# Two mixing layers in fp32 on one core: 22 of 50 weight slots as seven quarter-size products for eight, and attention's rounds in another order

## The chip, the core and the metric

The kernel runs on one core of a Trainium2 chip, in fp32. A core has five engines with queues of their own: TensorE (PE, matrix products into PSUM), VectorE (DVE), ScalarE (ACT), GpSimd (POOL) and SyncE (SP), which here only starts DMA transfers. They meet through semaphores: an instruction raises one when it ends, another engine waits for its value. The metric is the device time of one execution in microseconds, as the median of several. Less is better.

## The reference

The program is one block of another kind (a recurrent branch and latent attention) and then two equal layers over 272 tokens (16 learned ones and 256 of the input) of width 1024. The change concerns only the first part of these two layers, which I call the mixing stage:

```python
for l in range(2):
    n = rms_norm(h, mix_norm_g[l])
    q, k, v, qi, ki, wi, xr, yg, cv, gt = split(n @ w_in[l])
    q = rotary(rms_norm(q)); k = rotary(rms_norm(k)); qi = rotary(qi); ki = rotary(ki)
    # 8 small heads score the keys: sum_h wi[h] * relu(qi[h] . ki); the best 64 keys of a query stay
    attn = attention(q, k, v, kept keys)      # 8 heads of 128 over 2 groups of keys
    rnn  = scan(a_t * h + b_t) * gelu(yg)     # gates from two block-diagonal products of conv4(xr)
    cnv  = silu(layer_norm(conv31(cv_a * sigmoid(cv_g))))
    g_attn, g_rnn, g_conv = split(sigmoid(gt))
    merged = g_attn * (attn @ w_o_attn) + g_rnn * (rnn @ w_o_rnn) + g_conv * (cnv @ w_o_conv)
    h = h + merged @ w_out
    f = rms_norm(h, ffn_norm_g[l])
    h = h + (silu(f @ w_gate) * (f @ w_up)) @ w_down
```

conv31 and conv4 are causal convolutions of each channel by itself, over 31 and 4 tokens. Layer 1 leaves out the 16 learned tokens wherever only queries are needed, so its queries, gates, branches and output run over 256 columns.

## The kernel before

Features lie on the 128 partitions and tokens along the columns: a matrix of width 1024 is 8 tiles of 128 x 272. All weights come as one stream of slots of 1 MB (1024 rows by 256 outputs) in a ring of four (the order in LSTREAM; SyncE issues a slot's transfer at L501 once the slot four before it is used up, `slot_free`). One slot gives two output tiles of 128 features. `project` (L525 to L537) computes them plainly: for each tile 8 matmuls of 128x128 weights with 272 (or 256) columns, accumulated in one PSUM bank; four banks rotate, and ScalarE's `keep` (L769) copies each tile out.

The mixing stage of a layer takes 50 such slots after the small ones for qi, ki and wi: 8 for the inputs of the long convolution, 4 for q, 1 for k, 1 for v, 4 for xr, 4 for yg, 12 for the three gates, and then 4 each for the recurrent, the attention and the convolution branch and the output. TensorE's program is one fixed list. Between projections it has the small products: the index heads' logits; the sums of squares of heads (L605); the transposes of v; the 16 block-diagonal gate inputs of the recurrence (L618, between the YG and the gate projections); then attention in rounds (six in layer 0, four in layer 1): scores of four heads (L630), two or three gate slots, transposes of the weights (L637), and so on. The product with V comes after all rounds (L649: 8 heads, three key tiles each, 272 columns). Last come 32 tiles of branches and output (L676).

ScalarE copies, applies sigmoid, gelu, relu, exp and silu (the convolution's norm ends with eight Silu, L918, one a tile). Copies of transposed weights are at L893 and L897, those of attention's output at L910. VectorE does the index scores and the selection of 64 keys (`max` and `match_replace`, L1082), the long convolution (`conv_work`, L983 to L996: 124 steps, each two `scalar_tensor_tensor` of 272 elements, L995), the short one, the softmax parts (L1153, L1161), the scan, and in `vector_branches` (L1186 to L1207) the gating: one multiply from PSUM a tile (L1201) and one addition into MG (L1203). Its programs are lists too: `conv_until` says how many convolution steps stand between the parts. Sums over eight tiles are three additions on VectorE (`add_tiles`, L944, L946, L948) and one matmul with ones on TensorE (`sum_parts`, L521). GpSimd has no work in the mixing stage.

The feed-forward part uses a seven-product form (`products`, L730 for the gate and up quads, L754 for the last product). The 1024 x 256 weights of a slot are taken as 4 pairs of 2 x 2 blocks of 128, the tokens in two halves. VectorE or GpSimd make four sums of weight blocks (`weight_sums`, L954 to L959), VectorE four differences of token halves once for the whole input (`token_sums`, L965 to L970). Seven products of 4 matmuls with half the columns, 136 or 128, then replace eight. Every fourth result is copied by ScalarE (L934), and VectorE combines the rest out of three PSUM banks (`combine`, L1243 to L1250). There VectorE makes the sums of even slots and GpSimd those of odd ones.

## Time and profile before

| | |
|---|---|
| median of 3 runs | 1803.34 us |
| lowest and highest | 1799.0 and 1807.7 us |
| the profiled execution | 1804.26 us |
| span of its trace | 1802.5 us |
| mean granted clock of TensorE | 0.981 of 2.4 GHz |
| TensorE busy | 97% of the span |
| VectorE busy | 53% |
| ScalarE busy | 27% |
| GpSimd busy | 18% |

The profile is of one execution. The span is the time from its first to its last instruction; 1.8 us lie around it. Busy times are of instructions, without waits. A matmul's end is modelled, so a busy TensorE is not one at its best. In fp32 every matmul stands in the records as two instructions. The mixing stage of layer 0 lies between some 520 and 963 us of the span, its feed-forward part between 963 and 1170; layer 1 has its mixing stage between 1170 and 1598.

### The profile page before, as it was taken

The page shows a single profiled execution, that of the slowest core. Times are in us where ns is not written, and L with a number is a line of the kernel's source. Part 1 is how long each engine was busy: PE and PEld are TensorE (multiplying, and loading weights), DVE is VectorE, ACT ScalarE, POOL GpSimd, SP SyncE. Part 2 cuts the span into 40 slices and gives each one's busy share as a digit, 9 for nine tenths or more (in the row PEclk, how much of TensorE's full clock was granted, in tenths as well). Part 3 has the DMA queues.
Part 4 walks back from the last instruction along what each step waited for, and adds up shares of the span by engine and source line. Part 5 has one row for each costly group of instructions (what it writes and reads, how often), then busy time and mean ns, then how long its engine had stood idle before and what let it go on. Part 6 is the DMA issues. An engine that isn't in the chain of part 4 may idle for free.

```text
span 1802.5 us, 32221 instructions
## 1 busy us (share of the span) xinstructions
PE 1745.1 (97%) x13478; PEld 1448.9 (80%) x13478; DVE 954.9 (53%) x1913; ACT 492.4 (27%) x1064; POOL 329.4 (18%) x349
## 2 busy tenths in 40 slices
PE   6999998999999999999999999999999999989999
PEld 3345654898877888888888999978888888889999
DVE  2235335566446948565215765248667563157652
ACT  2123236344343134642111010041236322110000
POOL 0003300655100000000004564300000000036553
PEclk8999999799999999999999999999999999999999
DMA  8322300000334433333443444443344334334453
GB/s 320 123 93 97 117 20 1 4 4 4 121 140 140 140 120 139 139 117 117 140 140 124 162 163 164 162 144 137 140 140 141 140 107 151 141 140 164 165 174 106
DMA packets 53360, 225.46 MB, mean 125 GB/s; under 512 B 5088, under 2 KB 29024, under 8 KB 29280
## 3 DMA queue, kind: packets, MB, share of 16 engines
q1 hardware_dynamic: 53216, 223.40, 35.0%
q8 instruction: 107, 1.75, 0.4%
q14 instruction: 37, 0.30, 0.1%
HBM read 222.34 MB, written 1.05 MB: 124 GB/s over the span
## 4 chain that ended last, share of the span: by engine, by line
PE 90%; DVE 5%; ACT 3%; issue 1%; DMA 1%; DVEq 1%; SPq 0%; ACTq 0%
PE PS L535 26%; PE PS L730 14%; PE PS L676 13%; PE PS L1918 9%; PE PS L754 8%; PE PS L1415 2%; PE PS L1428 2%; PE PS L2016 1%; PE PS L548 1%; PE PS L649 1%; DMA ring<-stream_dram 1%; PE PS L1936 1%; PE PS L618 1%; PE PS L630 1%; PE PS L1863 1%
## 5 line engine op out<-in xcount | busy, mean ns | idle before, releaser
L535 PE MATMUL PS<-arena,ring 128*128 128x272 f32 (+1 forms) x2176 | 498.1, 389 | 0.0
L535 PEld LDWEIGHTS PS<-arena,ring 128*128 128x128 f32 x2176 | 411.2, 190 | 77.2 <-issue 1.4
L676 PE MATMUL PS<-arena,ring 128*128 128x272 f32 (+1 forms) x1024 | 229.5, 386 | 2.1 <-DVE arena L1203 2.1
L995 DVE SCALAR_TENSOR_TENSOR arena<-arena,par 128x272 f32<-128x272 f32 (+1 forms) x480 | 214.9, 489 | 16.4 <-issue 0.9
L676 PEld LDWEIGHTS PS<-arena,ring 128*128 128x128 f32 x1024 | 194.2, 190 | 36.0 <-DVE arena L1203 2.9
L954 POOL TENSOR_TENSOR arena<-ring 128x512 f32<-128x512 f32 (+1 forms) x32 | 39.9, 1248 | 1000.4 <-DMA ring<-stream_dram 1000.2
L730 PE MATMUL PS<-arena 128*128 128x136 f32 (+1 forms) x1280 | 156.1, 281 | 8.4 <-DVE arena L959 8.4
L1918 PE MATMUL PS<-arena,ring 128*128 128x512 f32 (+2 forms) x448 | 158.3, 514 | 1.7 <-DVEq L2233 1.7
L730 PEld LDWEIGHTS PS<-arena 128*128 128x128 f32 x1280 | 152.5, 195 | 8.8 <-issue 8.8
L1918 PEld LDWEIGHTS PS<-arena,ring 128*128 128x128 f32 (+1 forms) x448 | 84.0, 189 | 75.1 <-issue 69.1
L769 ACT ACTIVATE arena<-PS 128x272 f32<-128x272 f32 (+1 forms) x144 | 55.7, 393 | 323.6 <-PE PS L535 313.7
L730 PE MATMUL PS<-arena,ring 128*128 128x136 f32 (+1 forms) x960 | 116.1, 277 | 0.0
L730 PEld LDWEIGHTS PS<-arena,ring 128*128 128x128 f32 x960 | 112.6, 191 | 0.1
L754 PE MATMUL PS<-arena 128*128 128x136 f32 (+1 forms) x704 | 84.0, 277 | 0.0
L754 PEld LDWEIGHTS PS<-arena 128*128 128x128 f32 x704 | 81.9, 191 | 0.0
L754 PE MATMUL PS<-arena,ring 128*128 128x136 f32 (+1 forms) x528 | 64.3, 277 | 0.0
L754 PEld LDWEIGHTS PS<-arena,ring 128*128 128x128 f32 x528 | 62.1, 191 | 0.0
L1670 POOL TENSOR_TENSOR ring<-arena,H 128x256 f32<-128x256 f32 x64 | 45.7, 740 | 88.1 <-ACT arena L1589 88.0
L1243 DVE TENSOR_TENSOR arena<-PS,arena 128x272 f32<-128x272 f32 (+1 forms) x48 | 20.8, 433 | 70.7 <-ACT arena L940 42.2
L1201 DVE TENSOR_TENSOR arena<-PS,arena 128x272 f32<-128x272 f32 (+1 forms) x32 | 13.9, 433 | 80.6 <-PE PS L676 80.6
L2242 DVE TENSOR_SCALAR arena<-arena,smalls 128x512 f32<-128x512 f32 x14 | 11.1, 790 | 83.4 <-ACT arena L2088 83.4
L934 ACT ACTIVATE arena<-PS 128x136 f32<-128x136 f32 (+1 forms) x40 | 11.2, 281 | 154.3 <-PE PS L730 154.3
(360 smaller groups left out, 2359.0 us busy)
## 6 DMA issues: line engine op xcount, KB each, us to landing
ring<-stream_dram SPq DMA_DIRECT2D x185, 1024.0 KB, 4.8
ring<-stream_dram SPq DMA_DIRECT2D x32, 512.0 KB, 4.3
ring<-stream_dram SPq DMA_DIRECT2D x16, 384.0 KB, 3.8
arena<-x_dram SPq DMA_DIRECT2D x1, 2048.0 KB, 11.5
cst<-const_dram SPq DMA_DIRECT2D x1, 1080.0 KB, 7.7
out_dram<-H SPq DMA_DIRECT2D x4, 256.0 KB, 3.4
cst<-const_dram SPq DMA_DIRECT2D x1, 912.0 KB, 9.6
arena<-stream_dram SPq DMA_DIRECT2D x1, 512.0 KB, 7.7
```

What stands on the lines that cost most here:

```text
L535: last = mm(PS[:, (m + f) % 4, nw], lslot(l, n, KD, 256)[:, k, P * f:P * f + P], NT[:, k, nw], start=k == 0, stop=k == KD - 1)
L676: last = mm(PS[:, i % 4, NQ], lslot(l, n, KD, 256)[:, k, P * (i % 2):P * (i % 2) + P], src[:, k, NQ], start=k == 0, stop=k == KD - 1)
L730: last = mm(out, w[:, k], src[:, k] if tokens is None else src[:, k, tokens], start=k == 0, stop=k == 3)
L754: last = mm(out, w[:, i], src[:, k] if tokens is None else src[:, k, tokens], start=k == 0 and r in (0, 3, 5), stop=k == 10 and r in (2, 4 ...
L769: a(out, PS[:, m % 4, nw] if src is None else src, func, **more).then_inc(L["kept"], 1)
L954: e.tensor_tensor(to[:, 0], a21, a22, ALU.add)
L995: stt(CVG[:, c, NQ], CVA[:, c, j + Q0:j + T2], dw_w[l][:, c, j:j + 1], CVG[:, c, NQ], ALU.mult, ALU.add)
L1243: tt(to[:, 0:2], cb, over(CA[:, nth % 2, 0:nh], 2), ALU.add)
L1415: last = mm(PS[halves(h), 4 * d, 32 * q:32 * q + 32], XL[l - 1][halves(h), d, q, :], columns(ZW[halves(h), n % 2, d, 0, q, :], l, GROWN[d] ...
L1428: last = mm(PS[halves(h), 4 * d, 256 + 32 * q:288 + 32 * q], ZW[halves(h), n % 2, d, 1, q, :], P1[halves(h), d, 32 * q:32 * q + 32], start ...
L1670: tt(XL[l - 1][:, d], AS[:, d], over(level_mask(d, l), 4), ALU.mult).then_inc(S["xl_ready"], 1)
L1918: last = mm(out, weights(n, KD, 256)[:, k, P * f:P * f + rows], HT[:, k, lo:T1], start=k == 0, stop=k == KD - 1)
```

## The change

The 50 slots of the mixing stage get numbers j from 0 to 49 and one common loop on TensorE, one on ScalarE and one on VectorE. Their order is now q (0 to 3), k (4), two convolution inputs (5, 6), xr (7 to 10), v (11), the other six convolution inputs (12 to 17), yg (18 to 21), the gates of the recurrent and the attention branch (22 to 29), the recurrent branch (30 to 33), the gates of the convolution branch (34 to 37), the attention branch (38 to 41), the convolution branch (42 to 45), the output (46 to 49). 22 of them, MIXED, use seven products; the others stay plain.

**The seven-product form here.** A mixed slot has two PSUM banks. Its products run in the order a, g, c, h, b and, in the slot after it, e and d; a mixed slot that follows a mixed one interleaves them (a, e of the one before, g, c, d of the one before, h, b). The products a, c, e and d stand in one region one after the other, and each accumulates on the one before (c on a, e on c, d on e); g is the start of h. ScalarE copies a, g, c, e and d out, and a product that accumulates further waits for the copy of what stands there. VectorE combines with two operations, `sum_f0` and `sum_f1`. GpSimd makes the weight sums (`mix_sums`, four operations of 128 x 512 elements, double-buffered). The token differences are made once for each input: of the projections by VectorE and GpSimd, of attention's output by GpSimd (`att_halves`), of the convolution branch by VectorE (`conv_halves`), of MG by VectorE pair by pair (`merge_sums`).

**The rest.** Attention's rounds begin at slots 17, 20, 23, 26, 29 and 32 (four in layer 1): scores ahead of the slot, transposes in the next, and the product with V of that round in the one after (`attend`, all four heads of a group side by side, up to 512 columns); PT shrinks to one round. The gates lie in two buffers of 8 tiles instead of one of 24, their sigmoid is applied in place. The gate inputs of the recurrence stand in four parts ahead of and inside slots 14 and 15, on banks 4 to 7. Convolution steps are now given slot by slot (CONV_STEPS). The gating of branch slot j - 1 is the last thing VectorE does in its turn of slot j, ahead of the convolution's own sums. In TensorE's turn of slot j, `within` stands between d and h (in a mixed slot) or ahead of the second tile (in a plain one). The ring's order (LSTREAM) follows the new order. The feed-forward part and the first block stay.

```diff
+CV_J = (5, 6, 12, 13, 14, 15, 16, 17)
+SCORES = (17, 20, 23, 26, 29, 32)
+CONV_SUM_J = 37
+MIXED = [*range(2, 8), 11, 16, 20, 24, 28, 35, *range(OA_J, OC_J + 3), *range(WO_J + 1, MIXES)]
+CONV_STEPS = {8: 2, 9: 2, 10: 2, 11: 2, 13: 3, 14: 1, 15: 1, 16: 7, 17: 4, 18: 6, 19: 6, 20: 5, 21: 6, 22: 4, 23: 5,
+              24: 6, 25: 2, 26: 2, 27: 6, 28: 7, 29: 5, 30: 7, 31: 7, 32: 5, 33: 6, 34: 6, 35: 7, 36: 2}
...
+            def product_c(j):
+
+                summed(j, 2)
+                pe.wait_ge(L["copies"], B["copies"] + COPIES["a", j])
+                product(banks(j)[0], MS[MIXED.index(j) % 2][:, 1], operands(j)[2][1]).then_inc(L["products"], 1)
...
+            def within(j):
...
+                if j - 1 in SCORES[:len(R)]:
+                    turn_weights(SCORES.index(j - 1))
+                if j - 2 in SCORES[:len(R)]:
+                    attend(SCORES.index(j - 2))
...
+                if j == CONV_SUM_J + 2:
+                    pe.wait_ge(L["conv_sq_in"], B["conv_sq_in"] + 1)
+                    sum_parts(CSUM[:, 1], 5, NQ, L["conv_sq_sum"])
...
+            for j in range(MIXES):
+                before(j)
+                if j in MIXED:
+                    product_a(j)
+                    if j - 1 in MIXED:
+                        product_e(j - 1)
...
+                    if j == OC_J:
+                        pe.wait_ge(L["conv_halves"], B["conv_halves"] + 1)
...
+                    product_g(j)
...
+                    product_c(j)
+                    if j - 1 in MIXED:
+                        product_d(j - 1)
+                    within(j)
+                    product_h(j)
+                    product_b(j)
...
+                else:
+                    plain(j, 0, range(4))
+                    if j - 1 in MIXED:
+                        product_e(j - 1)
+                    plain(j, 0, range(4, 8))
+                    if j - 1 in MIXED:
+                        product_d(j - 1)
+                    within(j)
+                    plain(j, 1, range(8))
...
+                if j in CONV_STEPS:
+                    conv_work(done, done + CONV_STEPS[j])
+                    done += CONV_STEPS[j]
+                if j - 1 in BRANCH:
+                    gate(j - 1)
+                if j == CONV_SUM_J:
+                    add_tiles(v, CSUM[:, 0, NQ], CVG[:, :, NQ], CSQ[:, 0:4, NQ]).then_inc(L["conv_sum_in"], 1)
+                if j == CONV_SUM_J + 2:
                     dve.wait_ge(L["conv_sq"], B["conv_sq"] + 1)
                     add_tiles(v, CSUM[:, 1, NQ], CSQ[:, :, NQ], CSQ[:, 0:4, NQ]).then_inc(L["conv_sq_in"], 1)
...
+                if j == CONV_SUM_J + 4:
+                    dve.wait_ge(L["conv_out"], B["conv_out"] + 1)
+                    x = CVG.rearrange("p (k e) t -> p k e t", e=2)
+                    token_sums(v, x[:, :, 0], x[:, :, 1], TCNV, n0, n1).then_inc(L["conv_halves"], 1)
...
+            def mix_sums(i):
+
+                j = MIXED[i]
+                w11, w12, w21, w22 = quarters(l, mix_slot(j))
+                to = MS[i % 2]
+                lslot_wait(pool, l, mix_slot(j))
+                if i >= 2:
+                    pool.wait_ge(L["products"], B["products"] + PRODUCTS["b", MIXED[i - 2]])
+                g.tensor_tensor(to[:, 0], w21, w22, ALU.add).then_inc(L["summed"], 1)
+                g.drain()
+                g.tensor_tensor(to[:, 1], to[:, 0], w11, ALU.subtract).then_inc(L["summed"], 1)
+                g.drain()
+                g.tensor_tensor(to[:, 2], w12, to[:, 1], ALU.subtract).then_inc(L["summed"], 1)
+                g.tensor_tensor(w21, w11, w21, ALU.subtract).then_inc(L["summed"], 1)
```

## Rows read from the trace of the kernel before

**Rows 1.** The page, busy time by engine: microseconds, share of the span, instructions.

```profile
PE 1745.1 (97%) x13478; PEld 1448.9 (80%) x13478; DVE 954.9 (53%) x1913; ACT 492.4 (27%) x1064; POOL 329.4 (18%) x349
```

**Rows 2.** Waits of TensorE: waiting line, releasing line, microseconds in total, times, longest.

```profile
PE PS L676 <- DVE arena L1203: 2.1, 2, 1.1
...
PE PS L637 <- DVE arena L1161: 1.3, 1, 1.3
PE PS L649 <- ACT arena L910: 1.0, 2, 0.5
...
PE PS L618 <- ACT arena L769: 0.9, 2, 0.5
```

**Rows 3.** Timeline, ScalarE, layer 0: start, length, instruction, count, [idle before, releaser].

```profile
704.38 0.40 ACT L769 ACTIVATE arena<-PS 128x272 f32<-128x272 f32 x1 [3.27 <-PE PS L535]
```

**Rows 4.** Timeline, VectorE, two gated output tiles of layer 1.

```profile
1509.22 0.42 DVE L1201 TENSOR_TENSOR arena<-PS,arena 128x256 f32<-128x256 f32 x1 [2.51 <-PE PS L676]
...
1512.68 0.42 DVE L1201 TENSOR_TENSOR arena<-PS,arena 128x256 f32<-128x256 f32 x1 [2.51 <-PE PS L676]
```

**Rows 5.** Timeline, ScalarE, copies two quads apart, in layer 0 and layer 1.

```profile
1024.26 0.28 ACT L934 ACTIVATE arena<-PS 128x136 f32<-128x136 f32 x1 [6.20 <-PE PS L730]
...
1037.23 0.28 ACT L934 ACTIVATE arena<-PS 128x136 f32<-128x136 f32 x1 [6.20 <-PE PS L730]
...
1694.96 0.28 ACT L934 ACTIVATE arena<-PS 128x128 f32<-128x128 f32 x1 [5.97 <-PE PS L730]
...
1707.47 0.28 ACT L934 ACTIVATE arena<-PS 128x128 f32<-128x128 f32 x1 [5.98 <-PE PS L730]
```

**Rows 6.** Timeline, TensorE, from attention's product with V to the branches.

```profile
819.32 4.13 PE L649 MATMUL PS<-arena 128*128 128x272 f32 x24
...
828.01 1.36 PE L676 MATMUL PS<-arena,ring 128*128 128x272 f32 x5
```

**Rows 7.** Timeline, VectorE, the three additions of a sum over eight tiles.

```profile
825.66 1.29 DVE L944 TENSOR_TENSOR arena<-arena 128x1088 f32<-128x1088 f32 x1
827.03 0.72 DVE L946 TENSOR_TENSOR arena<-arena 128x544 f32<-128x544 f32 x1
827.83 0.44 DVE L948 TENSOR_TENSOR arena<-arena 128x272 f32<-128x272 f32 x1
```

**Rows 8.** Timeline, ScalarE, the table load and eight Silu of the convolution branch.

```profile
860.80 1.28 ACT L918 ACT_TABLE_LOAD   x1
865.53 4.14 ACT L918 ACTIVATE arena<-arena,par 128x272 f32<-128x272 f32 x8 [3.45 <-DVE arena L1193]
```

**Rows 9.** Timeline, VectorE, 21 steps of the long convolution in a row.

```profile
594.39 20.68 DVE L995 SCALAR_TENSOR_TENSOR arena<-arena,par 128x272 f32<-128x272 f32 x42
```

**Rows 10.** Timeline, weight sums of the feed-forward part, on VectorE and on GpSimd.

```profile
977.03 0.69 DVE L955 TENSOR_TENSOR arena<-ring 128x512 f32<-128x512 f32 x1
...
989.95 1.54 POOL L957 TENSOR_TENSOR arena<-arena,ring 128x512 f32<-128x512 f32 x1
990.28 1.75 DVE L955 TENSOR_TENSOR arena<-ring 128x512 f32<-128x512 f32 x1
```

**Rows 11.** Timeline, first block, a GpSimd and a VectorE operation at the same time.

```profile
166.02 4.68 POOL L2174 TENSOR_TENSOR arena<-arena 64x2048 f32<-64x2048 f32 x1 [116.71 <-DVE arena L2260]
...
166.41 4.84 DVE L2247 SCALAR_TENSOR_TENSOR arena<-arena,par 128x510 f32<-128x510 f32 x1
```

**Rows 12.** The page, DMA issues of 1 MB slots: count, size, median from issue to landing.

```profile
ring<-stream_dram SPq DMA_DIRECT2D x185, 1024.0 KB, 4.8
```

**Rows 13.** TensorE after a gap: timeline, then window with busy time, granted clock, DMA.

```profile
969.49 0.70 PE L730 MATMUL PS<-arena 128*128 128x136 f32 x4 [4.05 <-DVE arena L959]
...
969.50:974.00 4.50, 4.50 (x24) 0.62 0.17 66
```

**Rows 14.** Windows: busy PE, PEld, DVE, ACT, POOL; granted clock; DMA share; GB/s.

```profile
1050.00:1100.00 50.00, 50.00 (x434) 50.00 (x433) 34.83 (x51) 4.90 (x12) 28.96 (x30) 1.00 0.45 155
600.00:650.00 50.00, 50.00 (x220) 41.46 (x219) 39.21 (x86) 8.13 (x16) 0.00 (x0) 1.00 0.39 136
```

More of the change, by code:

```diff
@@ L233, in build @@
         Qb = cut(3536, KD, T2)
+        AT = Qb
         Kb = cut(5712, 2, T2)
@@ L525, in norm_sums @@
                 pe.wait_ge(L["added"], B["added"] + nth + 1)
[L526 to L537 removed]
+                sum_parts(SQN if nth else SQS, bank, nw, L["sums"])
             if l == 0:
@@ new lines, in scalar_layers, with width, copy_a @@
+            a(WT, PS[64:72, 6, NW], ACT.Copy)
+            for h in range(2):
+                last = a(KIb[halves(h), :], PS[0:64, 6, NW], ACT.Copy)
+            last.then_inc(L["kept"], 1)
+            def width(j):
+                n = mix_halves(l, j)[0]
+                return n.stop - n.start
+            def copy_a(j):
+                act.wait_ge(L["products"], B["products"] + PRODUCTS["a", j])
+                if MIXED.index(j) >= 2:
+                    act.wait_ge(L["mixes"], B["mixes"] + f0_at(j) - 4)
+                n = width(j)
+                a(copies(j)[0][:, 0, 0:n], PS[:, 2 * (j % 2), 0:n], ACT.Copy).then_inc(L["copies"], 1)
```

1031 lines of the change are left out of this document (693 added, 338 removed).

## The prediction

> **What bounds the kernel now.** I read the page's busy shares first: TensorE is busy 97% of the 1802.5 us span [rows 1], so time leaves this kernel only as matmul time or as a gap of TensorE. Then the waits of TensorE: in the two layers' mixing stage they are small, and those that the change takes away stand in [rows 2]. Then the pitch of the work, which counts better than a busy sum since matmul ends are modelled: the distance between two evictions of the same kind is the time of the matmuls between them. One output tile of 8 matmuls of 272 columns takes the 3.27 us that ScalarE waits for it and the 0.40 of its copy, so a plain slot of two tiles 7.33 us [rows 3]; with 256 columns 1512.68 - 1509.22 = 3.46, and 6.91 us a slot [rows 4]. The feed-forward part already uses the seven-product form: two slots take 12.97 us at 136 columns (6.49 each, 0.927 per product of 4 matmuls) and 12.51 us at 128 (6.26 each) [rows 5].
>
> **Part 1, fewer columns.** 22 slots a layer change form. Layer 0: 22 x (7.33 - 6.49) = 18.5 us. In layer 1 a mixed projection runs over all 272 tokens, though queries, YG and gates ran over 256: 6 slots gain 0.84 (one K, V, XR, three convolution inputs), 6 gain 6.91 - 6.49 = 0.42, and the 10 slots of branches and output gain 6.91 - 6.26 = 0.65: 5.0 + 2.5 + 6.5 = 14.0. Together **-32.5 us**. This is the most that the form can give.
>
> **Part 2, attention.** The product with V took 828.01 - 819.32 = 8.69 us in layer 0 [rows 6], a wait of 0.5 in it (L649 of [rows 2]). It becomes 10 matmuls of 512 columns and two of 64. By the step from 256 to 272 columns (0.0267 us a matmul) 512 columns are an estimated 0.86, so 9.1 against 8.2: +0.9, and +0.6 in layer 1: **+1.5**. Transposes, logits and scores stay in number.
>
> **Part 3, waits that go.** The four lines of [rows 2] have 2.1 + 1.3 + 1.0 + 0.9 = **-5.3 us**: outputs no longer wait for the last gate of MG, gate inputs lie among other tiles, and so do the transposes.
>
> Sum so far -36.3: without any new gap 1804.3 - 36.3 = 1768.0 in the profiled execution.
>
> **Part 4, gaps that the new order makes by itself.** I walked each slot with the durations of rows; T39 is the start of mix slot 39.
> Slot 39: TensorE issues a, e of 38, g, c, d of 38 and then, before h, waits for the convolution's squares to be added. VectorE's program has ahead of that sum the gating of slot 38, which needs d of 38, the product just issued. So: 5 products end at T39 + 4.6; copy by ScalarE until 5.0; two gate operations of 0.72 until 6.6; the three additions 1.29 + 0.72 + 0.44 with drains, 2.6 [rows 7], until 9.2 and more. Gap 4.8 us in layer 0, 4.5 in layer 1: **9.3**. Nothing hides it: TensorE's queue is in order, h and b of 39 are behind it.
> Slot 41: ScalarE has the eight Silu of slot 40, a table load of 1.28 and 4.14 us [rows 8], behind the copy of d of 39 (T40 + 5.0); it is free at T40 + 10.4 = T41 + 3.9, and only then copies a of 41, for which c waits from 2.8: 1.5 us a layer, **3.0**.
> Slot 42: its g waits for the sums of the convolution's halves, on VectorE behind gate 40 (T41 + 8.1) and four operations of 544 elements, 3.1 us, so until T42 + 3.2 against 1.85: **2.8** for two layers.
> Slot 33 of layer 0: its first tile needs the bank that gate 31 empties, which stands behind five convolution steps of 0.985 (20.68 us for 42 operations [rows 9]): **1.2**. End of the stage: d of 49 waits for a copy, and the last H comes one copy later: some 1.0 a layer, **2.0** (from the copy of 0.28 in [rows 5] and additions of 0.44). Sum **+18.3**.
> ScalarE's five copies a mixed slot, and combining on VectorE (an operation of 272 elements, 0.44 in [rows 7], and one of 136), are costed at nothing elsewhere: between a copied product and its next use lie one or two products of 0.93 us, and in the first run of six mixed slots the chain combine, scores, Relu, logits just fits by this walk (6.6 of 7.2 us). If that cover is gone, each is late by its own length, 0.3 to 0.7.
>
> **Part 5, VectorE against GpSimd.** The weight sums go to GpSimd, 4 operations and some 5.4 us for a mixed slot (each up to the 1.54 of [rows 10]), 44 x in all. What the trace shows is that the two engines take turns when both read two SBUF operands: a VectorE addition of 512 elements takes 0.69 us with GpSimd idle and 1.75 beside it, while GpSimd's takes 1.54 [rows 10]; the instruction of the convolution's kind, scalar_tensor_tensor, took 4.84 us under a GpSimd operation of 4.68 [rows 11], where [rows 9] have 0.49 for half the length. So within such a window of some 6 us VectorE does 4 operations, not 12, and loses about 4 us. The Trainium skill, page "SBUF — State Buffer", section "SBUF: two separate sides", calls the pair of ports an exclusive lock, kept for a whole instruction, with PSUM-reading operations outside it; by that rule the combining of the first half (it reads PSUM) is free and the rest of this part stands at its upper end, by the mean rows of both engines at about half.
> Where does that loss end last? A slot's load begins when the slot four before is free and lands 4.8 us later [rows 12]. Slot 35's sums so begin at T32 + 4.8, inside the five steps ahead of gate 31: layer 0 gains 4.3 us of gap in slot 33. In layer 1 attention is over early, so the sums of 35 are followed at once by the halves of AT, 8 operations in a row over the twelve operations of slot 33, and gate 32 is 6.5 us late for slot 34. In slots 41 and 42 the sums of 42 and 43 fall on gate 40 and on the four operations of the convolution's halves: 4 x 1.3 and some, 5.6 us in each layer. These four are **22.0**. The same walk gives 0 to 14 more in smaller pieces (first run, weights of rounds 2 and 3, slots 37, 39, 46); I take **2**, since gaps ahead of them give VectorE time. The whole part is between 0, if the windows fall on VectorE's idle time, and 36. A gain is excluded, since GpSimd did nothing in this stage (0.00 us of 50 in [rows 14]).
>
> **Part 6, the clock.** A gap of 4.05 us before 969.49 was followed by a granted clock of 0.62 over 4.5 us, half speed for 3.4 of them [rows 13], so 1.7 us. Six of my gaps are over 4 us: 0 to 12, taken at **6**, because a slower TensorE is also one that VectorE catches up with.
>
> **Sum:** 1804.3 - 36.3 + 18.3 + 22.0 + 2 + 6 = 1816.3 for the profiled execution; unprofiled medians lie 0.9 lower, so **1815 us**.
>
> **Rivals.** (a) *The gaps of part 5 don't come*: windows and VectorE's work miss each other, as GpSimd's four operations can also fall into its waits. Then part 5 is 0 and part 6 about 4: 1804.3 - 36.3 + 18.3 + 4 - 0.9 = 1789, and 1780 with part 4's gaps but slot 39's (9.0) also gone. For it: VectorE was idle for a fifth of the stretch of [rows 14] in this stage (busy 39.21 of 50 us). Against it: steps of 5 to 7 us are set against slots of 7.3. (b) *All of it comes*, VectorE and GpSimd are the bound of the whole stage: 36 and 12 give 1834. This one decides from the point where convolution steps plus GpSimd windows pass a slot's 7.33 us. (c) *The seven-product form doesn't run at its pitch here*: it reads its accumulators back between products, so each slot has five waits for ScalarE. At 0.1 us for each of 220 waits +22: 1837. Against it: the quads keep 6.49 with a copy and the same group length.
> (d) *The clock swings in the mixed runs*, since TensorE idles shortly at each of their waits. Against it: in this trace the quads, which change banks with their products as well, have a granted clock of 1.00 over 50 us [rows 14]. Were a fifth of 44 slots at half clock: 44 x 6.4 x 0.2 = +56, 1870. The Trainium skill, page "TensorE: Matmul & The Clock Gate", section "A second HAM failure mode: psum-queue depth-cycling", tells of a kernel in which such short idles at bank changes did let the clock swing; the row speaks against that rule for this form, so the chance is small.
>
> **How the numbers follow.** Forecast 0.44; (a) 0.35; (b) 0.11; (c) 0.07; (d) 0.03. Half a per cent, about what can be told from no change, is 1794 to 1812. Of the forecast case 0.02 lies below, 0.15 inside, 0.27 above; of (a) 0.28 below and 0.07 inside; the rest above. Faster 0.30, same 0.22, slower 0.48. The range reaches from (a) with the small gaps gone to (b): 1780 to 1834; the likeliest case alone is 1798 to 1828.
>
> **What will show it.** Part 1: evictions in mixed runs 6.5 us apart, and fewer matmul columns. Part 4: TensorE waits of 4 to 5 us, twice, for VectorE's third addition of the convolution's squares, ScalarE's Silu just before a wait of 1.5. Part 5: convolution operations of 1.3 to 1.7 us beside GpSimd's, TensorE waits for gate products in slot 33 or 34 and for the halves in slot 42. Part 6: granted clock under 1 behind them. I am wrong if VectorE's operations keep 0.49 beside GpSimd, or if TensorE's waits in the two stages sum to under 20 us.

## The result: 1838.07 us, slower by 1.8%

The changed kernel takes 1838.07 us (median of 4 runs, 1835.61 to 1840.69) beside 1805.52 us for the kernel before in the same comparison, a ratio of 1.0182 with a 95% interval of 1.0152 to 1.0212. The direction was forecast (1815 us as the likeliest time), the size was not, and the time lies 4 us above the stated range of 1780 to 1834.

The profiled execution took 1836.84 us with a span of 1835.1. The first part of its page answers to [rows 1]:

```profile
PE 1740.0 (95%) x14482; PEld 1471.1 (80%) x14482; DVE 1100.4 (60%) x1999; ACT 543.3 (30%) x1206; POOL 592.3 (32%) x537
```

TensorE's busy time fell by only 5 us (it holds the matmuls that ran at a lower clock, see below) and its idle time rose from 57 to 95 us. VectorE is busy 146 us longer for only 86 instructions more, and GpSimd 263 us longer.

The waits of TensorE, from 515 us on, with the columns of [rows 2]:

```profile
PE PS L670 <- DVE arena L1369: 20.2, 6, 4.9
PE PS L747 <- DVE arena L1622: 10.2, 3, 5.0
PE PS L704 <- DVE arena L1391: 8.2, 2, 4.2
PE PS L1008 <- DVE arena L1380: 5.0, 2, 2.5
PE PS L704 <- ACT arena L1098: 4.5, 4, 1.5
PE PS L853 <- DVE arena L1598: 2.0, 3, 1.2
PE PS L964 <- ACT arena L1344: 1.7, 2, 0.9
```

The lines of the new kernel: L670 is a sum over eight tiles by the matrix of ones, L1369 the last of VectorE's three additions for it; L747 is a plain slot, L704 a product of a mixed one; L1622 gates a branch slot, L1391 is the last of the convolution branch's four token differences, L1098 the copy of product a, L853 the transposes of attention's weights, L1344 the gain of a tile of H, L964 the first gate tiles of the feed-forward part. The large gaps in order of time, layer 0 and then layer 1, with the columns of [rows 3]:

```profile
815.03 5.55 PE L747 MATMUL PS<-arena,ring 128*128 128x272 f32 x16 [4.96 <-DVE arena L1622]
871.61 1.28 PE L670 MATMUL PS<-arena,c 128*128 128x272 f32 x2 [4.87 <-DVE arena L1369]
887.24 1.17 PE L704 MATMUL PS<-arena 128*128 128x136 f32 x8 [1.46 <-ACT arena L1098]
897.20 3.62 PE L704 MATMUL PS<-arena 128*128 128x136 f32 x16 [4.16 <-DVE arena L1391]
954.62 5.75 PE L964 MATMUL PS<-arena,ring 128*128 128x272 f32 x16 [0.88 <-ACT arena L1344]
964.41 0.72 PE L670 MATMUL PS<-arena,c 128*128 128x272 f32 x2 [4.04 <-DVE arena L1369]
...
1485.93 9.55 PE L747 MATMUL PS<-arena,ring 128*128 128x256 f32 x32 [4.74 <-DVE arena L1622]
1529.99 1.22 PE L670 MATMUL PS<-arena,c 128*128 128x256 f32 x2 [4.84 <-DVE arena L1369]
1545.38 1.13 PE L704 MATMUL PS<-arena 128*128 128x128 f32 x8 [1.51 <-ACT arena L1098]
1555.03 3.24 PE L704 MATMUL PS<-arena 128*128 128x128 f32 x16 [4.04 <-DVE arena L1391]
...
1619.51 1.22 PE L670 MATMUL PS<-arena,c 128*128 128x256 f32 x2 [3.94 <-DVE arena L1369]
```

These are slot 33 (34 in layer 1), 39, 41, 42 and the end of the mixing stage. Behind the gaps TensorE ran at its lower level of 1.2 GHz. Windows of the stretches right behind three of them, columns as in [rows 14]:

```profile
871.60:876.40 4.80, 4.79 (x19) 4.56 (x20) 1.18 (x1) 2.20 (x3) 0.00 (x0) 0.50 0.00 0
1530.00:1535.70 5.70, 5.70 (x27) 5.52 (x28) 2.18 (x1) 2.17 (x3) 0.93 (x1) 0.55 0.01 1
897.20:900.60 3.40, 3.40 (x16) 3.40 (x17) 1.20 (x2) 0.28 (x1) 1.08 (x1) 0.54 0.00 0
```

By length times 1 less the granted share TensorE lost 2.4, 2.6 and 1.6 us in them.

**A measure that is free of the first block.** The first block is the same program in all kernels here, but in the profiles TensorE loses between 15 and 31 us in it to the lower clock. So I compare, beside the medians, the stretch from the first sum of layer 0 (524.45 us before, 523.19 after) to the end of the span. In it I add up the gaps of TensorE over 0.25 us, and half of the time that TensorE was busy at the lower level (the loss by the clock). All times in us; "rest" is the stretch without gaps and loss. These four columns come from one profiled execution of each kernel, and the loss by the clock is the least steady of them: where the lower level came with a gap of 2.5 us or more, it lay between 1.4 and 3.1 us.

| kernel | ratio to before (95% interval) | stretch | gaps | lost by the clock | rest |
|---|---|---|---|---|---|
| before | 1 | 1278.0 | 17.1 | 3.9 | 1257.0 |
| changed | 1.0182 (1.0152 to 1.0212) | 1311.9 | 53.8 | 21.4 | 1236.7 |
| e1 all plain, new order | 1.0009 (0.9990 to 1.0028) | 1281.7 | 15.2 | 4.8 | 1261.7 |
| e2 small sums | 1.0044 (1.0030 to 1.0058) | 1287.0 | 36.7 | 15.3 | 1235.0 |
| e3 gate first | one run | 1314.2 | 55.9 | 21.0 | 1237.2 |
| e4 mended, 22 slots | 1.0019 (0.9996 to 1.0043) | 1282.9 | 37.8 | 12.0 | 1233.1 |
| e5 16 slots | 1.0146 (1.0118 to 1.0174) | 1305.4 | 43.7 | 16.7 | 1245.0 |
| e6 mended, 16 slots | 0.9946 (0.9926 to 0.9966) | 1271.6 | 24.7 | 6.3 | 1240.7 |
| e7 tail | one run | 1299.0 | 49.2 | 17.2 | 1232.6 |
| e8 squares first | one run | 1307.9 | 51.3 | 20.4 | 1236.3 |
| e9 e6, steered | 0.9932 (0.9910 to 0.9953) | 1271.4 | 22.5 | 9.6 | 1239.4 |
| e10 e9 and early sums | 0.9869 (0.9846 to 0.9892) | 1260.1 | 14.6 | 6.5 | 1239.1 |
| e11 e10 with 22 slots | 0.9876 (0.9853 to 0.9900) | 1258.6 | 20.2 | 6.3 | 1232.0 |
| e12 before, early sums | 0.9906 (0.9885 to 0.9927) | 1267.0 | 8.7 | 1.7 | 1256.6 |

So the change took 20.3 us off the rest, and put 36.7 us of gaps and 17.5 us of slow clock on top: +33.9.

### The profile page after: what moved, and what is told of

The parts are those of the page before. It is cut to its first block, busy times and chain, and to the rows that moved or that the text cites. A ratio compares the mean times of both kernels' runs of the same rounds, so it can differ in the third digit from the quotient of the medians.

```text
span 1835.1 us, 35365 instructions
## 1 busy us (share of the span) xinstructions
PE 1740.0 (95%) x14482; PEld 1471.1 (80%) x14482; DVE 1100.4 (60%) x1999; ACT 543.3 (30%) x1206; POOL 592.3 (32%) x537
## 4 chain that ended last, share of the span: by engine, by line
PE 84%; DVE 7%; ACT 3%; DVEq 2%; issue 1%; DMA 1%; ACTq 0%; SPq 0%
PE PS L747 18%; PE PS L1008 14%; PE PS L704 14%; PE PS L2487 9%; PE PS L1032 7%; PE PS L1984 2%; PE PS L1997 2%; DVE arena L1416 1%; DVEq L1418 1%; PE PS L686 1%; PE PS L2585 1%; PE PS L864 1%; PE PS L972 1%; PE PS L827 1%; DMA ring<-stream_dram 1%
## 5 line engine op out<-in xcount | busy, mean ns | idle before, releaser
L747 PE MATMUL PS<-arena,ring 128*128 128x272 f32 (+1 forms) x1792 | 422.4, 391 | 10.5 <-DVE arena L1622 10.2
L747 PEld LDWEIGHTS PS<-arena,ring 128*128 128x128 f32 x1792 | 338.2, 192 | 75.4 <-issue 15.9
L1416 DVE SCALAR_TENSOR_TENSOR arena<-arena,par 128x272 f32<-128x272 f32 (+1 forms) x480 | 252.3, 566 | 14.8
L1819 POOL TENSOR_TENSOR arena<-ring 128x512 f32<-128x512 f32 x44 | 65.9, 1498 | 510.7 <-DMA ring<-stream_dram 431.4
L704 PE MATMUL PS<-arena,ring 128*128 128x136 f32 (+1 forms) x1408 | 186.4, 281 | 0.7 <-ACT arena L1118 0.7
L704 PEld LDWEIGHTS PS<-arena,ring 128*128 128x128 f32 x1408 | 177.6, 193 | 6.4 <-issue 1.4
L1008 PE MATMUL PS<-arena 128*128 128x136 f32 (+1 forms) x1280 | 155.6, 281 | 5.0 <-DVE arena L1380 5.0
L1008 PEld LDWEIGHTS PS<-arena 128*128 128x128 f32 x1280 | 152.0, 194 | 5.4 <-issue 5.4
L704 PE MATMUL PS<-arena 128*128 128x136 f32 (+1 forms) x1056 | 139.3, 285 | 12.8 <-DVE arena L1391 8.2
L704 PEld LDWEIGHTS PS<-arena 128*128 128x128 f32 x1056 | 131.7, 196 | 16.0 <-DVE arena L1391 8.8
L1008 PE MATMUL PS<-arena,ring 128*128 128x136 f32 (+1 forms) x960 | 116.1, 277 | 0.0
L1008 PEld LDWEIGHTS PS<-arena,ring 128*128 128x128 f32 x960 | 112.6, 191 | 0.1
L1137 ACT ACTIVATE arena<-PS 128x272 f32<-128x272 f32 (+1 forms) x88 | 34.5, 393 | 230.6 <-PE PS L747 186.3
L1032 PE MATMUL PS<-arena 128*128 128x136 f32 (+1 forms) x704 | 84.0, 277 | 0.0
L1032 PEld LDWEIGHTS PS<-arena 128*128 128x128 f32 x704 | 81.9, 191 | 0.0
L2239 POOL TENSOR_TENSOR ring<-arena,H 128x256 f32<-128x256 f32 x64 | 45.7, 743 | 87.3 <-ACT arena L2158 87.3
L1506 DVE TENSOR_TENSOR arena<-arena 128x136 f32<-128x136 f32 (+1 forms) x44 | 25.1, 570 | 72.5 <-ACT arena L1118 72.4
L1032 PE MATMUL PS<-arena,ring 128*128 128x136 f32 (+1 forms) x528 | 64.3, 277 | 0.0
L1032 PEld LDWEIGHTS PS<-arena,ring 128*128 128x128 f32 x528 | 62.1, 191 | 0.0
```

The costliest lines, as they stand in the source:

```text
L704: last = mm(out, w[:, k], tokens[:, k], start=start and k == 0, stop=k == 3, skip_group_check=True)
L747: last = mm(PS[:, 2 * (j % 2) + f, nw], w[:, k, P * f:P * f + P], src[:, k, nw], start=k == 0, stop=k == KD - 1)
L1008: last = mm(out, w[:, k], src[:, k] if tokens is None else src[:, k, tokens], start=k == 0, stop=k == 3)
L1032: last = mm(out, w[:, i], src[:, k] if tokens is None else src[:, k, tokens], start=k == 0 and r in (0, 3, 5), stop=k == 10 and r in (2, 4 ...
L1137: a(plain_to(j, f)[:, nw], PS[:, 2 * (j % 2) + f, nw], ACT.Copy).then_inc(L["copies"], 1)
L1416: stt(CVG[:, c, NQ], CVA[:, c, j + Q0:j + T2], dw_w[l][:, c, j:j + 1], CVG[:, c, NQ], ALU.mult, ALU.add)
```

## Experiments

My theory after the result: the seven-product form gives about what was counted, the new order by itself costs little, and the loss is four late items and VectorE's shortage of time beside GpSimd, with the clock behind each gap. The rivals are the new order itself, contention as the one cause of all gaps, and the form with its copies.

### e1: all slots plain

```diff
-MIXED = [*range(2, 8), 11, 16, 20, 24, 28, 35, *range(OA_J, OC_J + 3), *range(WO_J + 1, MIXES)]
+MIXED = []
```

> The new order with no slot in the seven-product form: all 50 slots plain, GpSimd without weight sums in the mixing stage, everything else as in the changed kernel. Theory (the loss comes from mixed slots meeting the new order: late gates, copies and sums, and the clock behind the gaps): with plain slots of 7.33 us each of these chains has its cover again, so no gap over 2 us stays in the two mixing stages, and the time is that of the kernel before, 1803 us, plus 2 for attention, minus up to 5 for waits that go: 1798 to 1808. Rival (the new order by itself costs, through the places of convolution steps, rounds and sums): gaps of 4 to 5 us stay in slots 33, 39 and 42 and the time is over 1820.

Measured: 1807.77 us, ratio 1.0009, as the theory had it. The largest gap in the mixing stages is 1.21 us, apart from the 2.26 us at the start of layer 1 that every profile has; the two ahead of the first sum product stay, 4.42 and 4.33 us. The rest is 4.7 us above that of the kernel before: this is what the new form of the product with V and the order cost. The new order by itself isn't the cause; it only becomes tight when slots get shorter and GpSimd works beside VectorE.

### e2: GpSimd's sums made small

This kernel leaves out the weight sums of 120 of the 128 columns of each block, so it doesn't compute the layer; TensorE has the same matmuls.

```diff
-                g.tensor_tensor(to[:, 0], w21, w22, ALU.add).then_inc(L["summed"], 1)
+                g.tensor_tensor(to[:, 0, :, 0:8], w21[..., 0:8], w22[..., 0:8], ALU.add).then_inc(L["summed"], 1)
```

and so for the other three.

> As the changed kernel, but GpSimd's four weight sums of a mixed slot cover 8 of 128 columns of each block, so the sums that the products read are wrong and GpSimd is hardly busy. Theory (VectorE is held up by GpSimd in windows of 6 us, and that makes part of the gaps): the mean of a convolution step's operation falls from 566 to 490 ns; the gap of slot 33 in layer 0 falls from 5.0 to about 1.2, that of slot 34 in layer 1 from 4.7 to 0, those of slot 42 from 4.1 to 1.4, and those of slot 39 (4.8), of slot 41 (1.5) and ahead of the feed-forward sums (4.0) stay: 14 us of gaps and some 8 of the clock, so 1814 to 1820. Rival 1 (contention makes all of them): no gap over 2 us, under 1795. Rival 2 (contention costs nothing at the end): within 4 us of 1838.

Measured: 1813.17 us, ratio 1.0044, 25 us under the changed kernel and just under the range of the theory. The long convolution's operations, in the groups by line (busy time, mean in ns | idle before), in the changed kernel and then in e2:

```profile
L1416 DVE SCALAR_TENSOR_TENSOR arena<-arena,par 128x272 f32<-128x272 f32 (+1 forms) x480 | 252.3, 566 | 14.8
```

```profile
L1416 DVE SCALAR_TENSOR_TENSOR arena<-arena,par 128x272 f32<-128x272 f32 (+1 forms) x480 | 223.1, 506 | 14.8
```

The gap of slot 33 fell to 1.25, that of slot 34 in layer 1 to 1.73, those of slot 42 to 1.39 and 1.32; those of slot 39 (4.58 and 4.39), slot 41 (1.46 and 1.50) and the end (4.04 and 3.94) stayed. The operation of the convolution fell less than expected, to 506 and not 490 ns, and slot 34 isn't free of its gap. Gaps are down by 17.1 us and the clock's loss by 6.1. So contention is the cause of some 23 us, and others make the remaining gaps. Rival 1 falls, and rival 2 too.

### e3: the gate ahead of the convolution steps

```diff
+                if j - 1 in BRANCH:
+                    gate(j - 1)
                 if j in CONV_STEPS:
                     conv_work(done, done + CONV_STEPS[j])
                     done += CONV_STEPS[j]
-                if j - 1 in BRANCH:
-                    gate(j - 1)
```

> As the changed kernel, but VectorE gates slot j - 1 ahead of the convolution steps of its turn j (gates 30 to 33), not behind them. Theory (in slots 33 and 34 TensorE waits for a gate that only stands behind convolution steps in VectorE's list; the steps themselves are in no hurry): the gaps of 4.96 (layer 0) and 0.49 + 4.74 us (layer 1) for the gating go, with 3 to 5 us of the clock, and none comes in their place: 1823 to 1828. Rival (VectorE is short of time here, so the lateness only moves, to the convolution's sum in slot 37): a new gap of 3 us or more in slots 35 to 37, and 1833 or more.

Measured: 1833.61 us in one run, and the stretch is 2 us longer. The two gaps for the gating went, and a wait of 2.77 us for the weights' transposes in slot 33, one of 1.70 in slot 37 of layer 0 and one of 7.23 us in slot 37 of layer 1 came (timeline of TensorE, e3):

```profile
1505.87 1.19 PE L670 MATMUL PS<-arena,c 128*128 128x256 f32 x2 [7.23 <-DVE arena L1369]
```

My theory of the gate's place was wrong and the rival right: here VectorE is short of time, and an earlier gate only makes the convolution's last step later. The windows of the changed kernel say the same; VectorE is busy 45 of 50 us:

```profile
700.00:750.00 50.00, 50.00 (x283) 42.56 (x283) 45.73 (x82) 20.83 (x49) 9.74 (x7) 1.00 0.41 136
...
1350.00:1400.00 50.00, 48.75 (x251) 40.91 (x251) 45.24 (x78) 20.62 (x50) 12.48 (x8) 1.00 0.38 128
```

The first of these windows in the kernel before, in e1 and in e2:

```profile
700.00:750.00 50.00, 49.55 (x233) 39.77 (x233) 33.89 (x69) 29.82 (x74) 0.00 (x0) 1.00 0.38 135
```

```profile
700.00:750.00 50.00, 50.00 (x232) 39.85 (x231) 36.26 (x71) 19.83 (x44) 0.00 (x0) 1.00 0.36 127
```

```profile
700.00:750.00 50.00, 50.00 (x286) 42.17 (x285) 38.94 (x79) 22.89 (x55) 1.63 (x4) 1.00 0.37 127
```

So VectorE's 45.7 us are 36.3 of the new order with plain slots, some 2.7 more with mixed slots and small sums, and some 6.8 more with GpSimd's whole sums. These are near values: the windows don't begin at the same point of a slot, and the kernel before has another order.

### e4: six moves, no work left out

On ScalarE, at the end of the stage and in slot 41, and on GpSimd:

```diff
+                if j > WO_J:
+                    gain(*((0, 1), (1, 3), (3, 5))[j - WO_J - 1])
             copy_e(MIXES - 1)
             keep_d(MIXES - 1)
-            for k in range(KD):
+            gain(5, KD)
...
                     copy_g(j)
+                    if j == CONV_SUM_J + 4:
+                        open_conv(5, 8).then_inc(L["conv_out"], 1)
                     copy_c(j)
...
+                if j == OC_J + 1:
+                    pool.wait_ge(L["conv_halves"], B["conv_halves"] + 1)
```

`gain` holds the two operations on a tile of H, `open_conv` the Silu. On VectorE the gate goes ahead of the convolution steps as in e3, the additions of squares go ahead of the gating of slot 38, and the token differences of the convolution branch ahead of the gating of slot 40.

> The changed kernel with all its large gaps addressed by order alone, no work left out: gates ahead of convolution steps; the convolution's sum of squares ahead of the gating of slot 38; the feed-forward gains and squares of H spread over slots 47 to 49 instead of all behind the last copy; the last three of the eight Silu behind the first copies of slot 41; the convolution's halves ahead of the gating of slot 40, and GpSimd's sums of slot 43 behind them. Theory (each gap has its own late item; 58 us of gaps fall to about 22 and slow-clock stretches go with them): 34 us of gaps and some 12 of the clock less, 1788 to 1796, under the kernel before. Rival (one shared bound, VectorE beside GpSimd, which sends each gap elsewhere): 1815 or more.

Measured: 1809.75 us, ratio 1.0019, between theory and rival: neither number came. The stretch is 29.0 us shorter than that of the changed kernel: 16.0 of gaps, 9.4 of clock, 3.6 of rest. What I had missed is slot 37 of layer 1, as in e3:

```profile
1491.17 1.19 PE L670 MATMUL PS<-arena,c 128*128 128x256 f32 x2 [7.51 <-DVE arena L1381]
```

The gaps of slot 39 are 2.8 and those of slot 41 are gone, that of slot 42 went in layer 0 and is 1.06 in layer 1.

### e5: 16 mixed slots

```diff
-MIXED = [*range(2, 8), 11, 16, 20, 24, 28, 35, *range(OA_J, OC_J + 3), *range(WO_J + 1, MIXES)]
+MIXED = [*range(2, 8), *range(OA_J, OC_J + 3), *range(WO_J + 1, MIXES)]
```

> The changed kernel with 16 mixed slots in a layer: the six that stand singly among the plain ones (11, 16, 20, 24, 28, 35) are plain again. They bring TensorE 6 x 0.84 us in layer 0 and 3.4 us in layer 1, so 8.4, and take some 4 us each of VectorE's time. Theory (between slots 8 and 37 VectorE, over 90% busy, is the engine that is short, and GpSimd's windows there cost more than the six slots bring): the gaps of 5.0, 0.5 and 4.7 us in slots 33 and 34 fall to 1.2, 0.5 and 1.7, as with small sums, with 3 to 5 us of the clock; the gaps from slot 39 on stay. Time 1838 + 8.4 - 6.8 - 4 = 1832 to 1838, though 12 slots in all compute more. Rival (these windows are harmless and the gaps have another cause): the gaps stay and the time rises to 1844 to 1848.

Measured: 1831.27 us, ratio 1.0146. The stretch is 6.4 us shorter, though its rest is 8.3 us longer, where 8.4 were counted. The gaps of slot 33 and 34 fell from 5.0 to 1.2 and from 0.5 and 4.7 to nothing, the loss by the clock by 4.7. So the six single slots cost some 6 us more than they bring in this kernel by the stretch. By the times alone it isn't clear, since the intervals of the two ratios overlap.

### e6: mended, 16 slots

e4 with the list of e5, and two refinements, on VectorE and on ScalarE:

```diff
+                if j == CONV_SUM_J + 2:
+                    dve.wait_ge(L["conv_sq"], B["conv_sq"] + 1)
+                    add_tiles(v, CSUM[:, 1, NQ], CSQ[:, :, NQ], CSQ[:, 0:4, NQ]).then_inc(L["conv_sq_in"], 1)
                 if j - 1 in MIXED:
                     combine(j - 1)
...
             copy_e(MIXES - 1)
+            gain(5, 7)
             keep_d(MIXES - 1)
-            gain(5, KD)
+            gain(7, KD)
```

> The mended kernel (e4) with 16 mixed slots, the additions of the convolution's squares ahead of the combining of slot 38, and the gains and squares of H in a finer order at the end of the stage. Theory (VectorE short of time in slots 8 to 37): in e4 the lateness moved to slots 33 and 37 (2.5 and 1.7 us in layer 0, 0.5 and 7.5 in layer 1); without the six windows these four gaps fall under 1.5 in sum, that of slot 39 from 2.8 to about 1, the end of the stage from 1.5 to about 0.5, for 8.4 us of matmuls more and 5 us of the clock less: 1809.8 - 10.7 - 5.6 + 8.4 - 5 = 1797, from 1793 to 1801, under the kernel before. Rival (the gaps just move on again): 1808 or more.

Measured: 1795.64 us, ratio 0.9946: under the kernel before. The lateness in slots 33 and 34 is gone, slot 37 has 2.16 and 1.51 us (3.7, not under 1.5), slot 39 has 2.58 in layer 0 and none in layer 1.

### e7: only the end of the stage

Of e4's edits the one at the end of the stage alone.

> The changed kernel, only ScalarE's 16 operations on H (gain and square of eight tiles) spread: one tile in its turn of slot 47, two in 48, two in 49, three behind the last copy. Theory (they stood all behind the last copy, 5.8 us in a row, and so delayed the sums ahead of the feed-forward part): the waits of 0.9 and 4.0 us there fall to 0 and 1.5 in both layers, 6.7 us, with 1.5 to 5 us of the clock: 1826 to 1830. Rival (the last copy and addition of slot 49 make this wait): under 2 us in all, 1836 or more.

Measured: 1821.58 us in one run, stretch 12.8 us shorter, both more than expected. In the changed kernel ScalarE had all 16 operations behind the last copy (timeline of ScalarE):

```profile
953.78 0.28 ACT L1129 ACTIVATE arena<-PS 128x136 f32<-128x136 f32 x1 [1.28 <-PE PS L704]
953.97 0.51 ACT L1344 ACTIVATE arena<-H,par 128x272 f32<-128x272 f32 x1
954.38 0.42 ACT L1345 ACTIVATE arena<-H 128x272 f32<-128x272 f32 x1
...
959.49 0.42 ACT L1345 ACTIVATE arena<-H 128x272 f32<-128x272 f32 x1
```

5.9 us in a row, where the kernel before had all but the last tile's beside matmuls. With the edit the waits are 1.53 and 1.54 us and the 0.9 ahead of them is gone; 1.8 us of it came back in the next gap, ahead of the first sum product, which grew from 2.52 and 2.50 to 3.11 and 3.72. The rest fell by 4.0 us too: the first tile of 16 instructions behind the gap of 0.88 took 5.75 us (5.53 in layer 1) where it takes 3.83 (3.62) undisturbed, since it waited for its tiles of H one by one. These waits don't show as gaps, as ends are modelled, but the tile's pairs of instructions begin 0.73 us apart, as ScalarE's gains do in the rows above. The rival falls.

### e8: only the squares

The additions of squares moved behind `combine(38)`, ahead of its gating.

> The changed kernel, only VectorE's three additions of the convolution's squares moved ahead of the gating of slot 38. Theory (they are late because the gating waits for the product issued just before): the gap of 4.9 us in slot 39 falls to 2.8 in both layers, as in e4, 4.1 us, and some of the slow clock behind it (6.8 us at half speed in each layer) goes: 1830 to 1834. Rival (the squares of ScalarE are late, not the additions): the gap stays, 1838.

Measured: 1826.89 us in one run, but the stretch is only 3.9 us shorter; the rest of the difference to the changed kernel's profile, 6.0 us, lies ahead of it, in the first block, which is the same program. So the time confirms nothing here, only the gaps do. The gaps are 2.81 and 2.84, as expected; that of slot 42 in layer 1 rose from 4.0 to 5.4, and the clock gave back 1.0 us, less than I expected.

### e9: GpSimd kept off the critical additions

```diff
+                if j == OA_J:
+                    pool.wait_ge(L["conv_sum_in"], B["conv_sum_in"] + 1)
+                if j == OA_J + 2:
+                    pool.wait_ge(L["conv_sq_in"], B["conv_sq_in"] + 1)
```

and ScalarE's squares ahead of a sigmoid in slot 38.

> e6 with two waits more on GpSimd and one exchange on ScalarE: the weight sums of slot 38 begin behind VectorE's additions for the convolution's sum, those of slot 40 behind the additions of its squares, and ScalarE squares ahead of a sigmoid that nobody waits for yet. Theory (what is left in slots 37 and 39 is VectorE's additions and last steps beside GpSimd, 1.3 to 2.3 us an operation for 0.4 to 1.3; GpSimd has 6 to 10 us to spare there): the gaps of 2.16, 2.58 and 1.51 us go, and 1.7 us of the clock: 1795.6 - 8 = 1788, 1785 to 1791. Rival (GpSimd then is late itself): TensorE waits for weight sums in slots 38 to 41, 1794 or more.

Measured: 1794.32 us, ratio 0.9932, the stretch unchanged (1271.4 and 1271.6). The three gaps went, as expected, but slot 42 rose from 0.89 and 1.19 to 2.95 and 3.02 us, with slow clock behind each. GpSimd's delayed sums now lie on all four of the convolution's token differences in layer 0, which take 1.63 to 1.79 us each, where in e6 two of the four took 0.72 and 0.73. Neither side had it: the time is in the rival's range, but TensorE doesn't wait for the sums; the gain was lost two slots later.

### e10: weight sums of the first quad earlier

```diff
             add_tiles(v, SQN[:, NQ], SQ2[:, :, NQ], SQ2[:, 0:4, NQ]).then_inc(L["added"], 1)
+            even_sums(0)
             dve.wait_ge(L["root"], B["root"] + 2)
...
-            even_sums(0)
...
-            pool.wait_ge(L["gate_made"], B["gate_made"] + 1)
+            pool.wait_ge(L["halves_made"], B["halves_made"] + 1)
```

> e9, and at the start of the feed-forward part VectorE makes the weight sums of the first quad while it waits for the root, and GpSimd begins with its own behind VectorE's token differences. Theory (the gap of 3.6 and 4.2 us ahead of the first sum product is 16 operations of VectorE and then its four weight sums, half of them beside GpSimd): both gaps go, and the 10 us of slow clock behind them, 5 us: 1788 - 7.9 - 5 = 1775, 1771 to 1780. Rival (the sums only displace the root's users): the gap moves ahead of the second gate tile or quad, 1784 or more.

Measured: 1781.10 us, ratio 0.9869. That is 13.2 us under e9, where 13 were expected; the range was missed by 1 us because e9 hadn't reached its 1788. Both gaps ahead of the first sum product went, none came in their place, and the stretch is 11.3 us shorter. It is, with e11, the fastest kernel of the study: by the ratio some 24 us under the kernel before, and 57 under the changed one. What is left of waits from 515 us on:

```profile
PE PS L704 <- DVE arena L1404: 6.1, 3, 3.0
PE PS L670 <- DVE arena L1382: 4.2, 4, 2.3
PE PS L704 <- ACT arena L1098: 1.6, 2, 1.0
PE PS L792 <- ACT arena L1147: 1.1, 2, 0.5
```

### e11: the same with 22 slots

> e10 with all 22 mixed slots. Theory (between slots 8 and 37 a mixed slot costs VectorE more than it gives TensorE): 8.4 us of matmuls less, but waits for the weights' transposes in slot 33 and for the convolution's sum in slot 37 again, 5 to 14 us with the clock behind them: 1778 to 1784, not under e10. Rival (with GpSimd kept off the critical additions the six slots pay): 1766 to 1770.

Measured: 1783.14 us, ratio 0.9876, the stretch 1.5 us shorter than e10's: 7.1 of rest less, 5.7 of gaps more (2.72 in slot 33, 0.57 and 1.26 at other transposes, 4.21 for 3.04 in slot 42). The two can't be told apart. The six slots neither pay nor cost once the late items are mended.

### e12: the early sums in the kernel before

The edit of e10, nothing else.

> The kernel before with only the feed-forward edit of e10, nothing of the change. It measures what a gap of 4 us costs by itself: the two gaps of 4.05 and 4.39 us go. Theory (a gap of over 4 us also costs the clock that follows it): the 3.4 and 6.8 us at half speed behind them go too, 8.4 + 5.1 = 13.5 less, ratio 0.9925, from 0.990 to 0.995. Rival (the clock falls there for another reason, as the start of the seven-product form): the slow stretches stay and the ratio is 0.9955.

Measured: 1789.20 us, ratio 0.9906. The gaps of 4.05 and 4.39 us went, and so did the slow clock behind them (a window of e12 across that place; before, the 4.5 us behind the gap had 0.62 in [rows 13]):

```profile
955.00:975.00 20.00, 20.00 (x162) 19.49 (x161) 12.77 (x20) 1.94 (x5) 14.51 (x15) 1.00 0.56 206
```

That lies in the range of the theory. The stretch is 11.0 us shorter: 8.4 of gaps, 2.2 of clock (a new slow piece at 1165 us took some 1.7 of 3.9 back). The rival falls: the lower level there came with the gap, not with the form. It also says how e10 is to be read: 11 of its 18 us on this stretch come from an edit that has nothing to do with the change; the mended mixed slots bring the other 6.9. (The intervals of the two ratios just overlap, so these 6.9 rest on the stretches.)

## Why the prediction was wrong

On the stretch the prediction had -32.5 + 1.5 + 37.0 (new gaps 42.3, old waits -5.3) + 6 = +12.0 us; it measured +33.9. The difference of 21.9 us, by terms:

- **Part 6, the clock, +11.5: the step that failed.** It measured 17.5 where 6 was taken and 12 was my upper end. I had six gaps over 4 us, and halved their price, "because a slower TensorE is also one that VectorE catches up with". The six came (slots 33, 34, 39 and 42), and the loss behind them was 1.5 to 2.6 us each, 12.4 in all: the upper end, so the halving took off 6.4 us that were there. Nor did a slow TensorE help a later slot where it can be compared: the lower level behind slot 39 lasted 3.4 us in some profiles and 6.8 in others (e3, e5, e7 and the changed kernel), and the wait of slot 42 was 4.04 to 4.17 us in all of them. The other 5.1 us lie where I had no price: behind the two waits of 4.0 us at the end of the stage, behind those of 2.5 us ahead of the first sum product and behind the 2.26 us at the start of layer 1, 9.0 us less the 3.9 of the kernel before. The price of 1.7 us for a gap came from a single row [rows 13] and was low as well; the other gap of the kind in the kernel before, of 4.39 us at 1604 us, was followed by this window, a loss of 6.9 x 0.32 = 2.2:

```profile
1604.10:1611.00 6.90, 6.87 (x42) 6.90 (x43) 1.15 (x4) 0.28 (x1) 5.29 (x5) 0.68 0.06 23
```

- **Part 4, the end of the stage, +8.0.** I had 2.0 us, "one copy later", and didn't walk what ScalarE has behind that copy: 16 operations (e7). The waits are 0.37 + 0.88 + 4.04 and 0.37 + 0.85 + 3.94, less the 0.8 that were there before, and 3.8 in the drawn-out gate tile, 13.4; the next gap, ahead of the first sum product, shrank from 4.05 and 4.39 to 2.5 twice, -3.4. The change moves a loop behind a copy that waits for the last product, and I counted only the copy.
- **Part 2, +3.2.** e1 has 4.7 us of rest more, not 1.5. The product with V takes 10.45 us in layer 0 and 9.73 in layer 1 there, where the kernel before had 8.21 and 8.00 without its waits: 4.0 us more, not 1.5. The estimate of 0.86 us for a matmul of 512 columns is right where it has 128 keys. But the last key tile has 16, and its matmul takes longer. A round with two tiles and one with three in e1 (each matmul is two instructions, and the distance of the starts is its time):

```profile
743.81 2.07 PE L864 MATMUL PS<-arena 128*128 128x512 f32 x4
745.81 3.93 PE L747 MATMUL PS<-arena,ring 128*128 128x272 f32 x16
...
797.03 2.93 PE L864 MATMUL PS<-arena 128*128 128x512 f32 x6
799.89 3.93 PE L747 MATMUL PS<-arena,ring 128*128 128x272 f32 x16
```

  Two matmuls take 2.00 us and three 2.86, so one over 128 keys 0.86 and the last, with the change to it, 1.14. The remaining 0.7 us aren't placed.
- **Part 5 and the rest of part 4, -4.5.** Slot 33 came at 4.96 (5.5 forecast), slot 34 of layer 1 with its forerunner at 5.2 (6.5), slot 42 at 4.16 and 4.04 (7.0 each), together -7.6; slot 39 is 0.4 more, the small gaps are 3.5 for 2, and of the waits of [rows 2] that of L637 stayed, now as L853 with 1.25 us. The mechanism is as described, and e2 confirms each place: without GpSimd's windows slot 33 has the 1.25 and slot 42 the 1.4 of part 4. Slot 42 was too large because three of VectorE's six operations met a window, at 0.9 to 1.1 us each, where I had priced four at 1.3 and some.
- **Part 1, nearly right, +3.7.** Evictions in mixed runs are 6.48 us apart (941.10 and 947.58), e5 and the changed kernel differ by 8.3 us of rest, for 8.4 counted. But from e1, all plain, to e7, where the end of the stage is mended, the rest falls by 29.1 us, not by 32.5. The 3.7 us that are missing in the changed kernel may be waits under 0.25 us for copies, which no run here isolates, and stay open.
- **Slots 39 and 41, right**: 4.87 and 4.84 where 4.8 and 4.5 stood, 1.46 and 1.51 where 1.5 stood.

The sum: 11.5 + 8.0 + 3.2 - 4.5 + 3.7 = 21.9. That the new gaps as a whole came as forecast (36.7 us, less the old ones, for 37.0) is luck: those of part 5 were too large by as much as the end of the stage was too small.

Of the rivals, (a) falls: the windows did meet VectorE's work, and e2, which takes them away, still needs 1813.17 us and not 1789, since the end of the stage and the clock stay; (b) gave 1834 and was nearest, but for another reason, since part 5 didn't reach 36; (c) falls with the 6.48 us between evictions, and with e2, where the form runs with its copies and the copies' waits are 0.4 to 1.5 us in a few places; (d) falls too. A mixed run of the changed kernel has 1.00 beside gaps of 0.3 us at most:

```profile
925.00:950.00 25.00, 24.71 (x179) 22.99 (x178) 13.09 (x23) 3.69 (x13) 10.77 (x9) 1.00 0.43 149
```

That speaks, for this form, against the swing that the Trainium skill, page "TensorE: Matmul & The Clock Gate", section "A second HAM failure mode: psum-queue depth-cycling", tells of another kernel.

## What to carry to other kernels

When a form makes slots on the busiest engine shorter, walk every list that ran in the shadow of the long slots to its end, loops behind the last copy included: the engine with the least free time (here VectorE, 45 of 50 us) decides, and where it has none, moving one item only moves the gap (e3, e9; e7 and e8 did gain). Here a gap of 4 us on TensorE cost about 6 with the clock behind it; take such a price from several rows. Look for such gaps in the kernel as it is before adding a form: one moved call and one changed wait (e12) gave 11 us, and the mixed slots, once mended, 7.

## What the runs showed of the hardware that I had not expected

**The port pair of VectorE and GpSimd, operation by operation.** In the changed kernel, slot 42 (VectorE's four differences) beside GpSimd's sums, and a VectorE operation that reads PSUM. First the latter, under a GpSimd operation:

```profile
876.66 2.14 POOL L1819 TENSOR_TENSOR arena<-ring 128x512 f32<-128x512 f32 x1 [9.00 <-PE PS L704]
```

```profile
877.74 0.44 DVE L1498 TENSOR_TENSOR arena<-PS,arena 128x272 f32<-128x272 f32 x1
```

Then the differences, and the GpSimd operations beside them:

```profile
891.27 0.72 DVE L1386 TENSOR_TENSOR arena<-arena 128x544 f32<-128x544 f32 x1
891.90 1.81 DVE L1387 TENSOR_TENSOR arena<-arena 128x544 f32<-128x544 f32 x1
893.78 1.63 DVE L1389 TENSOR_TENSOR arena<-arena 128x544 f32<-128x544 f32 x1
895.49 1.66 DVE L1391 TENSOR_TENSOR arena<-arena 128x544 f32<-128x544 f32 x1
```

```profile
891.34 1.79 POOL L1819 TENSOR_TENSOR arena<-ring 128x512 f32<-128x512 f32 x1 [2.29 <-PE PS L704]
893.29 1.54 POOL L1821 TENSOR_TENSOR arena<-arena,ring 128x512 f32<-128x512 f32 x1 [0.16 <-issue]
```

An operation of two SBUF operands takes 1.63 to 1.81 us for 0.72, that is about its own time and the one GpSimd operation beside it, while the one from PSUM keeps its 0.44 under GpSimd. The Trainium skill, page "SBUF — State Buffer", section "SBUF: two separate sides", says so (an exclusive lock for a whole instruction, against VectorE operations with two SBUF inputs); the trace agrees.

**The clock also falls behind gaps of 2 to 3 us, but not always.** The same wait of 2.26 us at the start of layer 1 (2.26 or 2.27 in all 14 profiles) was followed by the lower level in seven of them and by full speed in the others. The windows right behind it, in the changed kernel and in e6:

```profile
1189.50:1194.00 4.50, 4.50 (x13) 3.65 (x14) 3.08 (x17) 2.86 (x6) 0.00 (x0) 0.62 0.01 4
```

```profile
1173.80:1178.30 4.50, 4.50 (x21) 3.96 (x22) 3.03 (x17) 3.22 (x7) 0.00 (x0) 1.00 0.00 0
```

Gaps of 2.9 us or more in the two layers were followed by the lower level, or had it begin inside them, in every profile; one of 2.72 us (e11, slot 33) was not. And the first block, the same program each time, lost 15 us to the clock in some profiles and 31 in others, so single executions can differ by that alone: those of the kernel before lie between 1799.0 and 1810.7 us.
